# One 2 MB transfer for an expert's gate and up weights in place of two of 1 MB

## The chip, the cores and the metric

The kernel runs on one core of one Trainium2 chip. The metric is the device time of one execution in microseconds (us). Of the kernel before, three runs were timed: 683.28, 684.06 and 685.25 us, the median is 684.06.

## What is computed

One step of a decoder layer over 544 tokens (512 of a prompt, 32 new ones) of width 1024: first a mixer (a spatial gating branch and a recurrent branch, merged by sigmoids and projected), then a mixture of experts, then a norm. The change touches the experts alone. Each of the 32 experts has a gate and an up matrix of 1024 x 256 and a down matrix of 256 x 1024 in float32, and each token goes to two of them:

```python
pg_top, g_idx = lax.top_k(pg, 1)
pe_top, e_idx = lax.top_k(pe, TOP_K_INNER)          # 2 of the 8 experts of the group
h = jax.nn.silu(jnp.einsum('td,edf->tef', xf, w_gate)) * jnp.einsum('td,edf->tef', xf, w_up)
h = h * gates.astype(h.dtype)[..., None]
y = jnp.einsum('tef,efd->td', h, w_down)
```

## The kernel before

The mixer takes the first 375 us or so. Its projection weights come in transfers of 512 KB over the queue of SyncE (SP).

Then routing builds a table of token numbers, and the experts are worked off in pairs. A pair G is two experts with up to 64 tokens each, which lie in the two halves of the 128 partitions. 16 pairs cover the 32 experts; an expert with over 64 tokens gets an extra pair with one half only. The inputs give one such extra, so there are 17 pairs, G = 0 to 16, and the extra one is G = 15.

For a pair, GpSimd gathers 128 token rows of 4 KB from DRAM into `xg` (`gather`, L538). TensorE transposes them (`transposes`, L1434), multiplies by gate and up (L1445: eight steps `c` of the inner dimension for two halves are 16 calls, which the trace shows as 32 matmuls), ScalarE and VectorE make `hm`, TensorE transposes that (L1456) and multiplies by down (L1466), ScalarE evicts to `yo` (L753), and GpSimd scatters the rows of `yo` to DRAM (`scatter`, L548). TensorE's order is written out: gate and up of G, transposes of G+1, down of G, gate and up of G+1, and so on. GpSimd's order is: wait for the transposes of G+1, gather G+2, wait for `yo` of G, scatter G, wait until that has landed, next G. The buffers `xg` and `yo` exist once.

The weights lie in `wslot[q][s]`: q = 0 to 2 are three slots for pairs, s is the half. An expert's 24 KB per partition are contiguous in DRAM: 16 KB of gate and up, interleaved by inner step `c`, and 8 KB of down. They come over SP's queue in the three parts of `PARTS`, each 1 MB in 128 rows of 8 KB: `c` 0 to 3, `c` 4 to 7, down. Six experts are loaded ahead (`expert`, L398): two near 115 us, one near 323 us, one near 367 us, one at 376 us, the last at 403.5 us. Afterwards `refill` (L440) refills the slot of each finished pair, part by part: it waits for `gu_half` (TensorE is past `c` = 3), loads part 0 of both experts, waits for `gu_mm` (past `c` = 7), loads part 1 of both, waits for `pair_mm` (past down), loads both down parts. `further` (L456) does the same for the one expert of the extra pair. Each part has its semaphore, and TensorE waits for part 0 ahead of `c` = 0, for part 1 ahead of `c` = 4 and for the down part ahead of L1466.

SP issues in program order, and the rows of one queue are worked off in order by the 16 DMA engines. The gathers and scatters have a queue of their own, which GpSimd fills, on the same 16 engines.

Behind the last pair, SP loads all of `ytok` back (`gy`), and VectorE, ScalarE and the stores make the output.

Of the kernel before, what the change touches and what calls it, by code (L numbers as in the profile page):

```python
# [97 lines left out]
def build(nc, x, wmix, wgate, chan, wst, bs, rows, wr, br, wmoe, y, vp, vs, st):  # L98
# [9 lines left out]
    GU = KT * 512  # L108
    EW = GU + 2 * D
# [124 lines left out]
    with ExitStack() as ctx:  # L234
        ps = ctx.enter_context(nc.psum_tensor("ps", [P, 8, 512], F32))

        def sem(name):
            return ctx.enter_context(nc.semaphore(name))
# [3 lines left out]
        const_in = sem("const_in")  # L242
        raw_in = [sem(f"raw_in{s}") for s in range(RAW)]

        part_in = [[[sem(f"part{n}_in{q}{s}") for s in range(2)] for q in range(3)] for n in range(3)]
        gw_in = sem("gw_in")
        xres_in = sem("xres_in")
        bd_in = sem("bd_in")
# [73 lines left out]
        coly_copied = sem("coly_copied")  # L322
        xgT_mm = sem("xgT_mm")
        xgT_sb = sem("xgT_sb")
        gu_half = sem("gu_half")
        gu_mm = sem("gu_mm")
        silu_done = sem("silu_done")
        hm_ready = sem("hm_ready")
# [2 lines left out]
        pair_mm = sem("pair_mm")  # L331
# [22 lines left out]
            return ([0, 1, 2, 5], 6, 4) if half == 0 else ([7, 3, 0, 1], 2, 2)  # L354

        TB = (5, 7, 4, 6, 5, 7, 4, 6)
        PARTS = ((0, GU // 2), (GU // 2, GU), (GU, EW))
        ZB = (4, 5, 2, 3)
        XB = (4, 6, 4, 6, 4, 6, 7, 3)

# [2 lines left out]
        def _(sp_):  # L363
# [31 lines left out]
            def expert(q, s, n):  # L395

                for part, (lo, hi) in enumerate(PARTS):
                    e.dma_start(wslot[q][s][:, lo:hi], wmoe[n][:, lo:hi]).then_inc(part_in[part][q][s], 16)  # L398
# [33 lines left out]

            def refill(q, count, number):

                for part, used in enumerate((gu_half, gu_mm, pair_mm)):
                    lo, hi = PARTS[part]
                    e.wait_ge(used, count)
                    e.sem_inc(held, 1)
                    for s in range(2):
                        e.dma_start(wslot[q][s][:, lo:hi], wmoe[bass.ds(number + s, 1), :, lo:hi].rearrange(  # L440
                            "a p c -> (a p) c")).then_inc(part_in[part][q][s], 16)

            with e.Fori(0, 4) as i:
                for q in range(3):
                    refill(q, i * 3 + (q + 1), i * 6 + (6 + 2 * q))
# [3 lines left out]

            def further(count, m):  # L450
                ex = e.value_load(nxi[0:1, bass.ds(m + 1, 1)], min_val=0, max_val=NE - 1)
                for part, used in enumerate((gu_half, gu_mm, pair_mm)):
                    lo, hi = PARTS[part]
                    e.wait_ge(used, count)
                    e.sem_inc(held, 1)
                    e.dma_start(wslot[0][0][:, lo:hi], wmoe[bass.ds(ex, 1), :, lo:hi].rearrange(  # L456
                        "a p c -> (a p) c")).then_inc(part_in[part][0][0], 16)

            with e.If(nx > 0):
                further(PAIRS - 3, 0)  # L460
            refill(1, PAIRS - 2, NE - 2)
            with e.If(nx > 1):
                with e.Fori(1, nx) as m:
                    further(m + (PAIRS - 1), m)
# [722 lines left out]
        def _(pe):  # L1187
# [241 lines left out]
            def transposes(G):  # L1429

                pe.wait_ge(xg_in, G * 16 + 16)
                pe.wait_ge(xgT_sb, FIRST + G)
                for c in range(KT):
                    l = pe.transpose(ps[:, c // 4, (c % 4) * P:(c % 4 + 1) * P], xg[:, c * P:(c + 1) * P], ident[:])  # L1434
                l.then_inc(xgT_mm, 1)

            def pair(G, q, halves, weights_in, next_rows):
                pe.wait_ge(xgT_sb, FIRST + G + 1)
                pe.wait_ge(hm_ready, FIRST + G)
                for c in range(KT):  # L1440
                    if c % 4 == 0:
                        for s in halves:
                            pe.wait_ge(part_in[c // 4][q][s], weights_in)
                    for s in halves:
                        l = pe.matmul(ps[CAP * s:CAP * s + CAP, 2, :], xgT[:, c, CAP * s:CAP * s + CAP],  # L1445
                                      wslot[q][s][:, c * 512:(c + 1) * 512], start=c == 0, stop=c == KT - 1,
                                      tile_position=(0, CAP * s), skip_group_check=True)
                    if c == 3:
                        l.then_inc(gu_half, 1)
                l.then_inc(gu_mm, 1)  # L1450
                if next_rows:
                    transposes(G + 1)
                pe.wait_ge(hm_ready, FIRST + G + 1)
                pe.wait_ge(hT_sb, FIRST + G)
                for f in range(2):
                    l = pe.transpose(ps[:, 3, f * P:(f + 1) * P], hm[:, f * P:(f + 1) * P], ident[:])  # L1456
                l.then_inc(hT_mm, 1)
                pe.wait_ge(hT_sb, FIRST + G + 1)
                for s in halves:
                    pe.wait_ge(part_in[2][q][s], weights_in)  # L1460
                pe.wait_ge(yo_sb, FIRST + G)
                for f in range(2):
                    for h in range(2):
                        for s in halves:
                            o = GU + f * D + h * 512
                            l = pe.matmul(ps[CAP * s:CAP * s + CAP, 6 + h, :], hT[:, f, CAP * s:CAP * s + CAP],  # L1466
                                          wslot[q][s][:, o:o + 512], start=f == 0, stop=f == 1,
                                          tile_position=(0, CAP * s), skip_group_check=True)
                l.then_inc(pair_mm, 1)

            transposes(0)
            with pe.Fori(0, PAIRS // 3) as i:
                for q in range(3):
                    pair(i * 3 + q, q, (0, 1), i * 16 + 16, True)
            pe.wait_ge(extra_ready, 1)
            nx = pe.value_load(nxi[0:1, 0:1], min_val=0, max_val=EXTRA)
            with pe.If(nx > 0):
                with pe.Fori(0, nx) as m:
                    pair(m + (PAIRS - 1), 0, (0,), m * 16 + 16 * (PAIRS // 3 + 1), True)
            pair(nx + (PAIRS - 1), 1, (0, 1), 16 * (PAIRS // 3 + 1), False)  # L1480


# [55 lines left out]
```

## Time and profile before

| | us |
|---|---|
| median of three runs | 684.06 |
| the profiled execution | 682.99 |
| its span | 681.0 |
| around the span | 1.99 |
| TensorE matmul busy | 572.9 |
| VectorE, ScalarE, GpSimd busy | 295.5, 242.6, 64.0 |
| share of 16 DMA engines used by SP's queue | 53.5% |
| mean granted TensorE clock, share of full | 0.941 |

The table is of one execution, taken by the hardware profiler. A line of the page's second part has 40 digits, one for each fortieth of the span (17.0 us); a digit is the busy share in tenths. A matmul counts as busy from its start to a modelled end, so that a busy TensorE is not one at its peak. A wait is put down to what released it last. In rows such as `407.06 8.58 PE L1445` the numbers are the start in us from the span's start and the length in us; in brackets stands how long the engine had been idle before and what ended that. "MATMUL x32" is a run of 32 merged instructions.

### The profile page before, as it was taken

How to read it: one execution, taken by the hardware profiler on the slowest of the kernel's cores; microseconds unless marked ns; L12 is line 12 of the kernel's file. 1: busy time of each engine (PE TensorE's matmuls, PEld its weight loads, DVE VectorE, ACT ScalarE, POOL GpSimd, SP SyncE). 2: the span in 40 equal slices, each digit the busy share in tenths (PEclk: the TensorE clock that was granted, in tenths of full speed). 3: DMA queues.
4: the chain of work that ended last, by engine and by line, in shares of the span. 5: the costliest groups of instructions: out<-in, count | busy, mean ns of one | idle time of the engine just before them, and what ended most of it. 6: DMA issues, size and time to landing. Idle time of an engine off the chain costs nothing.

```text
span 681.0 us, 8485 instructions
## 1 busy us (share of the span) xinstructions
PE 572.9 (84%) x2668; PEld 342.4 (50%) x2668; DVE 295.5 (43%) x583; ACT 242.6 (36%) x386; POOL 64.0 (9%) x137
## 2 busy tenths in 40 slices
PE   3899899999999999999998129898888988889800
PEld 3666497777778777777665113333333323223300
DVE  4824667767767667676323740110011000001138
ACT  5323324464573754654133401222222221112222
POOL 1100070000000000000000011112211221111000
PEclk9899999999999999999999659989999998889965
DMA  9322233921223222311903929999999999999464
GB/s 310 120 66 89 66 115 133 391 101 62 72 69 98 92 69 92 100 62 54 385 1 142 359 103 395 418 422 420 420 420 422 420 420 422 421 420 417 174 247 173
DMA packets 32001, 156.31 MB, mean 230 GB/s; under 512 B 6160, under 2 KB 6544, under 8 KB 19312
## 3 DMA queue, kind: packets, MB, share of 16 engines
q1 hardware_dynamic: 25744, 143.10, 53.5%
q0 software_dynamic: 5472, 10.63, 4.3%
q10 hardware_dynamic: 768, 2.38, 0.9%
q8 instruction: 9, 0.15, 0.1%
q14 instruction: 8, 0.07, 0.0%
HBM read 150.82 MB, written 14.17 MB: 242 GB/s over the span
## 4 chain that ended last, share of the span: by engine, by line
PE 55%; DMA 15%; SPq 15%; DVE 8%; issue 3%; ACT 3%; POOLq 0%; POOL 0%; DVEq 0%; ACTq 0%
PE ps L1192 13%; SPq L440 13%; PE ps L1194 12%; PE ps L1193 12%; DMA wslot<-in_wmoe 4%; DMA ytok<-yo,coly 4%; DMA xg<-xnd,colg 4%; PE ps L1466 3%; PE ps L1219 2%; PE ps L1308 2%; PE ps L1340 2%; DVE x L1173 2%; PE ps L1445 2%; SPq L456 1%; PE ps L1292 1%
## 5 line engine op out<-in xcount | busy, mean ns | idle before, releaser
L1445 PE MATMUL ps<-wslot,xgT 128*64 128x512 f32 x528 | 128.3, 621 | 11.4 <-DMA wslot<-in_wmoe 9.8
L589 ACT ACTIVATE wh<-raw 128x1024 fp32r<-128x1024 f32 x48 | 50.8, 1059 | 171.5 <-PE ps L1194 100.0
L1192 PE MATMUL ps<-xh,wh 128*128 128x512 f32 x256 | 102.5, 401 | 0.0
L1194 PE MATMUL ps<-xl,wh 128*128 128x512 f32 x256 | 100.0, 391 | 0.0
L1193 PE MATMUL ps<-xh,wl 128*128 128x512 f32 x256 | 99.9, 390 | 0.0
L1148 DVE TENSOR_TENSOR hm<-hs,ps 128x256 f32<-128x256 f32 x17 | 7.2, 421 | 197.0 <-ACT hs L748 197.0
L1445 PEld LDWEIGHTS ps<-wslot,xgT 128*64 128x64 f32 x528 | 42.2, 143 | 93.9 <-issue 93.9
L774 DVE TENSOR_TENSOR wl<-raw,wh 128x1024 fp32r<-128x1024 f32 x48 | 59.4, 1238 | 62.4 <-ACT wh L589 61.5
L1466 PE MATMUL ps<-wslot,hT 128*64 128x512 f32 x264 | 65.5, 627 | 8.3 <-ACT hT L750 8.3
L1192 PEld LDWEIGHTS ps<-xh,wh 128*128 128x128 f32 x256 | 48.1, 188 | 16.1 <-issue 6.7
L1194 PEld LDWEIGHTS ps<-xl,wh 128*128 128x128 f32 x256 | 48.1, 188 | 10.5
L1193 PEld LDWEIGHTS ps<-xh,wl 128*128 128x128 f32 x256 | 48.2, 188 | 9.4
L748 ACT ACTIVATE hs<-ps 128x256 f32<-128x256 f32 x17 | 6.5, 383 | 105.8 <-PE ps L1445 105.8
L753 ACT ACTIVATE yo<-ps 128x1024 f32<-128x1024 f32 x17 | 17.4, 1024 | 67.4 <-PE ps L1466 67.4
L1466 PEld LDWEIGHTS ps<-wslot,hT 128*64 128x64 f32 x264 | 19.2, 142 | 43.7 <-issue 31.4
L1434 PE MATMUL ps<-ident,xg 128*128 128x128 f32 x136 | 19.5, 288 | 16.9 <-DMA xg<-xnd,colg 16.9
L1434 PEld LDWEIGHTS ps<-ident,xg 128*128 128x128 f32 x136 | 15.3, 145 | 30.5 <-DMA xg<-xnd,colg 25.6
L1192 PE MATMUL ps<-wh,xh 128*128 128x512 f32 x64 | 27.3, 427 | 2.8 <-DVE xs L800 2.1
L1143 DVE TENSOR_TENSOR xgT<-ps,ch 128x1024 f32<-128x1024 f32 x17 | 20.8, 1225 | 19.5 <-PE ps L1434 19.5
L1192 PE MATMUL ps<-wh,mh 128*128 128x512 f32 x64 | 25.9, 405 | 0.2 <-DVE x L964 0.2
L1193 PE MATMUL ps<-wh,xl 128*128 128x512 f32 x64 | 26.0, 406 | 0.0
L1194 PE MATMUL ps<-wl,xh 128*128 128x512 f32 x64 | 25.9, 405 | 0.0
(290 smaller groups left out, 746.7 us busy)
## 6 DMA issues: line engine op xcount, KB each, us to landing
wslot<-in_wmoe SPq DMA_DIRECT2D x99, 1024.0 KB, 23.9
raw<-in_wmix SPq DMA_DIRECT2D x48, 512.0 KB, 3.6
gy<-ytok SPq DMA_DIRECT2D x8, 512.0 KB, 6.4
xt<-in_x SPq DMA_DIRECT2D x4, 512.0 KB, 7.1
x<-in_x SPq DMA_DIRECT2D x4, 512.0 KB, 4.8
xnd<-xn ACTq DMA_DIRECT2D x4, 512.0 KB, 9.1
out_y<-xn SPq DMA_DIRECT2D x4, 512.0 KB, 2.6
gw<-in_wgate POOLq DMA_DIRECT2D x8, 128.0 KB, 2.4
```

The lines of the kernel that those rows point to most:

```text
L440: e.dma_start(wslot[q][s][:, lo:hi], wmoe[bass.ds(number + s, 1), :, lo:hi].rearrange("a p c -> (a p) c")).then_inc(part_in[part][q][s], 16)
L589: a.activation(wh[:, hslot, :], raw[:, slot, :, :].rearrange("p k c -> p (k c)"), ACT.Copy).then_inc(hi_ready, 1)
L753: a.activation(yo[:], ps[:, 6:8, :].rearrange("p b c -> p (b c)"), ACT.Copy).then_inc(yo_sb, 1)
L774: d.tensor_tensor(wl[:, hslot, :], raw[:, slot, :, :].rearrange("p k c -> p (k c)"), wh[:, hslot, :].bitcast(F32), ALU.subtract).then_inc( ...
L1143: d.tensor_tensor(xgT[:], ps[:, 0:2, :].rearrange("p b (k c) -> p (b k) c", c=P), ch[:, :, C_G2:C_G2 + 1].broadcast_to([P, KT, P]), ALU.mu ...
L1173: d.scalar_tensor_tensor(out=x1[0:r, t, :], in0=gy[0:r, s, t, :], scalar=gate[0:r, s, t:t + 1], in1=x1[0:r, t, :], op0=ALU.mult, op1=ALU.a ...
L1192: pe.matmul(out, sh, mh_, start=start, stop=False)
L1193: pe.matmul(out, sl, mh_, start=False, stop=False)
L1194: return pe.matmul(out, sh, ml_, start=False, stop=stop)
L1434: l = pe.transpose(ps[:, c // 4, (c % 4) * P:(c % 4 + 1) * P], xg[:, c * P:(c + 1) * P], ident[:])
L1445: l = pe.matmul(ps[CAP * s:CAP * s + CAP, 2, :], xgT[:, c, CAP * s:CAP * s + CAP], wslot[q][s][:, c * 512:(c + 1) * 512], start=c == 0, st ...
L1466: l = pe.matmul(ps[CAP * s:CAP * s + CAP, 6 + h, :], hT[:, f, CAP * s:CAP * s + CAP], wslot[q][s][:, o:o + 512], start=f == 0, stop=f == 1 ...
```

## The change

`PARTS` has two entries in place of three: 16 KB per partition of gate and up, and 8 KB of down. So an expert comes in a transfer of 2 MB with 128 rows of 16 KB and one of 1 MB with 128 rows of 8 KB. The semaphore `gu_half` and its increment go, and both gate and up parts of a slot are reloaded after `gu_mm`. TensorE waits once, ahead of `c` = 0. The bytes, the slots and the order of everything else stay.

```diff
-        part_in = [[[sem(f"part{n}_in{q}{s}") for s in range(2)] for q in range(3)] for n in range(3)]
+        part_in = [[[sem(f"part{n}_in{q}{s}") for s in range(2)] for q in range(3)] for n in range(2)]
-        gu_half = sem("gu_half")
-        PARTS = ((0, GU // 2), (GU // 2, GU), (GU, EW))
+        PARTS = ((0, GU), (GU, EW))
             def refill(q, count, number):
-                for part, used in enumerate((gu_half, gu_mm, pair_mm)):
+                for part, used in enumerate((gu_mm, pair_mm)):
             def further(count, m):
-                for part, used in enumerate((gu_half, gu_mm, pair_mm)):
+                for part, used in enumerate((gu_mm, pair_mm)):
             def pair(G, q, halves, weights_in, next_rows):
                 for c in range(KT):
-                    if c % 4 == 0:
+                    if c == 0:
                         for s in halves:
-                            pe.wait_ge(part_in[c // 4][q][s], weights_in)
+                            pe.wait_ge(part_in[0][q][s], weights_in)
...
-                    if c == 3:
-                        l.then_inc(gu_half, 1)
                 l.then_inc(gu_mm, 1)
...
-                    pe.wait_ge(part_in[2][q][s], weights_in)
+                    pe.wait_ge(part_in[1][q][s], weights_in)
```

## Rows read from the trace of the kernel before

**Rows 1.** The page: TensorE and DMA busy tenths, GB/s, in 40 slices

```profile
PE   3899899999999999999998129898888988889800
...
DMA  9322233921223222311903929999999999999464
GB/s 310 120 66 89 66 115 133 391 101 62 72 69 98 92 69 92 100 62 54 385 1 142 359 103 395 418 422 420 420 420 422 420 420 422 421 420 417 174 247 173
```

**Rows 2.** Waits from 400 us on: engine, line, released by; total us, times, longest

```profile
POOL colg L540 <- DMA ytok<-yo,coly: 93.6, 11, 9.2
...
PE ps L1434 <- DMA xg<-xnd,colg: 16.9, 8, 7.7
...
PE ps L1445 <- DMA wslot<-in_wmoe: 9.8, 7, 2.5
```

**Rows 3.** TensorE's timeline: transposes L1434 of G = 1, 2, 11 and gate/up L1445

```profile
407.06 8.58 PE L1445 MATMUL ps<-wslot,xgT 128*64 128x512 f32 x32 [1.60 <-DVE xgT L1143]
415.57 1.09 PE L1434 MATMUL ps<-ident,xg 128*128 128x128 f32 x8
...
427.94 1.09 PE L1434 MATMUL ps<-ident,xg 128*128 128x128 f32 x8
...
551.52 1.09 PE L1434 MATMUL ps<-ident,xg 128*128 128x128 f32 x8 [1.05 <-DMA xg<-xnd,colg]
```

**Rows 4.** TensorE's timeline later: L1434 of G = 13, 14, 16, and waits of L1445

```profile
585.54 1.10 PE L1434 MATMUL ps<-ident,xg 128*128 128x128 f32 x8
...
597.04 5.35 PE L1445 MATMUL ps<-wslot,xgT 128*64 128x512 f32 x16 [2.50 <-DMA wslot<-in_wmoe]
602.32 1.09 PE L1434 MATMUL ps<-ident,xg 128*128 128x128 f32 x8
...
629.29 1.09 PE L1434 MATMUL ps<-ident,xg 128*128 128x128 f32 x8
...
638.53 3.65 PE L1445 MATMUL ps<-wslot,xgT 128*64 128x512 f32 x16 [0.25 <-DMA wslot<-in_wmoe]
```

**Rows 5.** Chain of work, 455 to 500 us: start, length, what

```profile
470.04 1.09 PE ps L1434 x8
...
471.83 3.68 PE ps L1466 x16
475.53 1.03 ACT yo L753
...
477.86 9.23 DMA ytok<-yo,coly
...
488.76 8.27 DMA xg<-xnd,colg
...
497.07 1.09 PE ps L1434 x8
```

**Rows 6.** The gather issued at 399.4 us: from issue to landing

```profile
DMA to landing us min/median/max: 4.0/4.0/4.0
```

**Rows 7.** The gather issued at 475.2 us, and all 17 gathers: from issue to landing

```profile
L543 POOL DMA_INDIRECT xg<-xnd,colg x1: 1037/1037/1037, 475.2 to 475.2; - x1
...
DMA to landing us min/median/max: 8.8/8.8/8.8
...
DMA to landing us min/median/max: 4.0/8.3/8.8
```

**Rows 8.** Transfers of gw (128 rows of 1 KB) issued at 115.0 and 142.0 us

```profile
DMA to landing us min/median/max: 6.4/6.4/6.4
...
DMA to landing us min/median/max: 2.3/2.3/2.3
```

**Rows 9.** Stretches: us; busy of PE, PEld, DVE, ACT, POOL; clock, DMA share, GB/s

```profile
408.00:410.00 2.00, 2.00 (x8) 0.73 (x6) 0.00 (x0) 0.00 (x0) 0.00 (x0) 0.50 1.01 426
412.00:414.00 2.00, 2.00 (x12) 0.77 (x10) 0.00 (x0) 0.00 (x0) 0.00 (x0) 1.00 0.88 271
...
480.00:500.00 20.00, 16.64 (x86) 6.56 (x84) 3.29 (x4) 3.84 (x6) 2.40 (x4) 1.00 1.02 421
```

**Rows 10.** SP's timeline, 402 to 413 us: the last preload and the first refill

```profile
403.51 1.28 SPq L398 DMA_DIRECT2D wslot<-in_wmoe  x3
412.47 0.34 SPq L440 DMA_DIRECT2D wslot<-in_wmoe  x1
```

**Rows 11.** Refills issued from 500 to 590 us: SP's time for one, issue to landing

```profile
L440 SPq DMA_DIRECT2D wslot<-in_wmoe x32: 332/2265/6664, 502.8 to 588.0; - x32
...
DMA to landing us min/median/max: 28.2/30.6/34.5
```

## The prediction

> **What bounds the kernel now.** I read the slices first [rows 1]: the change acts from 400 us on, where DMA stands at 9 and moves 417 to 422 GB/s through twelve slices. TensorE is also at 9 there, so the two have to be told apart, and the waits do that [rows 2]: matmuls waited for weights 7 times, 9.8 us in all, the transposes for gathered rows in 8 waits (7.7 us of them the very first), and GpSimd spent 93.6 us waiting for its own scatters. Then I read TensorE's timeline. From G = 1 (415.57) to G = 11 (551.52) the ten pairs take 13.6 us each and no gate/up waits for weights; the pair ends on the transposes, which wait for the gather [rows 3]. TensorE alone could do a pair in 12.4 us (G = 1 to G = 2, without a wait). Later pairs wait for weights ahead of `c` = 4 and take 16.8 us (585.54 to 602.32), until the last load lands and the last half of gate/up starts at 638.53 after a wait of 0.25 us only [rows 4].
>
> So there are two limits: a loop of gather and scatter, 13.6 us a pair, while the preloaded slots last, and the DMA stream after that. A pair's weights are 6 transfers of 1.05 MB, 14.9 us at 421 GB/s [rows 9]; gather and scatter are 1.05 MB more if every row counts, 2.5 us. That brackets the 16.8. SP is far ahead: refills issued from 502 us on land 28 to 34 us later, and SP itself is held up to 6.7 us in issuing one [rows 11].
>
> **The gather and scatter loop.** The rows of one turn are: a gather issued at 475.22 lands 8.8 us later, at 484.0 [rows 7]; the scatter issued at 477.86 lands at 487.1, thus 3.1 us behind the gather, since both use one queue [rows 5]; 1.7 us later, at 488.76, GpSimd issues the next gather. 8.8 + 3.1 + 1.7 = 13.6. TensorE's part (transposes, down, `yo`) runs beside the gather. The loop is therefore paced by how long 4 KB rows need on engines that are full of weight rows. The gather that met an idle DMA took 4.0 us, the median one 8.3 us [rows 6, 7]: 4.3 us more. The small load `gw` shows the same, 2.3 us alone and 6.4 us beside 8 KB weight rows, 4.1 us more [rows 8]. Both have 8 rows per DMA engine. At 421 GB/s over 16 engines a row of 8 KB lasts 0.311 us, so 8 small rows that each let one weight row pass lose 2.5 us; the other 1.8 us passes ahead of the first small row. This is the reading on which the forecast rests: the queues take turns row by row. (The Trainium skill, DMA: Bandwidth & Descriptors, section Queues, rings and completion order, has each DMA engine go round the queues it has work for and switch only between packets. If its packet of 9 to 17 descriptors were the unit, a change of row size would cost as much again ahead of the first row; no row here tells the two apart.)
>
> **The change, part by part.**
>
> 1. Rows of 16 KB pass in the small rows' gaps, 0.62 us each in place of 0.31. A gather that meets only such rows is longer by 8 x 0.31 = 2.5 us at least, and by the full 4.3 us if the part ahead of the first row grows too. The scatter's landing behind the gather grows by 2.5 us. So the loop would be 13.6 + 5.0 = 18.6 us (up to 20.4). Two thirds of the weight bytes come in such rows: 13.6 + 2/3 x 5.0 = 16.9 us, and 18.1 us with the upper price. No row shows 16 KB rows; the lower bound is no growth at all (13.6, a rival below). This is above the mean engine's work, 14.9 + half of 2.5 = 16.1 us, so backlog no longer builds up, the stream runs dry for a part of each period, and small rows then wait for nothing. With a loop of 6.6 us on an idle DMA (4.0 + 0.9 + 1.7; the 0.9 is an estimate, the slowest engine's eight rows at half weight and some landing), 7.0 us more when 8 KB rows are always there and 12.0 to 13.8 us more when 16 KB rows are, a period p with 5.4 us of the one and 10.7 us of the other solves p = 6.6 + (7.0 x 5.4 + 12.0 x 10.7) / p, 16.6 us, and 17.3 us with the upper price. Should gathers fall mostly beside down weights, p comes to about 15. I take 16.5.
>
> 2. The transposes of G = 1 stand at 415.57, just behind gate/up of G = 0. Their gather runs beside the last preloaded expert, now in 16 KB rows: up to 2.5 us later, I take 2.0, thus 417.6.
>
> 3. From G = 1 to G = 14, 13 periods of 16.5 = 214.5 us, to 632.1. The last refill is issued as gate/up and down of G = 13 end, so the gather of G = 15 still meets it (15 us), that of G = 16 hardly (12.4 us, TensorE's own). The transposes of G = 16 start at 659.5, where they started at 629.29: 30.2 us later. Weights are there by then, which saves the 0.25 us. Behind it nothing changes.
>
> 4. Both gate and up parts are refilled after `gu_mm` in place of `gu_half`. The first refill was issued at 412.47, halfway through gate/up that ends at 415.64 [rows 3, 10]: 3.2 us later now, at a place where the DMA had already a gap (0.88 busy at 412 to 414) [rows 9]. In the stream's limit it costs 3.2 us; under the longer loop it is hidden, as there is 16.1 us of work for 16.5. What is queued behind this wait on SP is the down refill, which waits for a later event anyway.
>
> 5. TensorE waits ahead of `c` = 0 for all 16 KB. For the last pair, whose second part landed last, that puts the first 16 matmuls, 3.5 us (half of 7.0), behind the landing. Again a cost of the stream's limit alone; in the forecast the landing is early.
>
> 6. 33 transfers and as many SP issues fewer. SP waits anyway, so nothing. One end price per row saved is bounded by the best stretch, 426 against 421 GB/s [rows 9]: 1.2% of the 226 us from 412 to 638, 2.7 us, hidden by the loop; at least zero.
>
> 7. The mixer: loads ahead of 400 us carry the same bytes with slack of many us behind them. Nothing.
>
> 8. With 4 us of idle time a pair TensorE may start some transposes and downs at the lower clock, as the gate/up of 5.35 us in place of 3.6 did behind a wait of 2.5 us [rows 4]. About 2 us a pair, beside the gather: nothing, unless the loop is shorter than I think.
>
> Sum: 681.0 + 30.2 - 0.25 = 710.9 us of span, 712.9 with the 1.99 around it. The median of the runs lies 1.07 above the profiled 682.99, so 714 us. Ends: with 17.3, a start at 418.1 and 15.5 and 12.8 for the last two pairs the transposes of G = 16 are at 671.3, 42 us late: 726; some clock loss on top, 730. With 15 they are at 640.0, the stream's limit and TensorE's end nearly meet, and 695 results.
>
> **The rivals.**
>
> - Rows of 16 KB don't hinder small rows more than 8 KB ones (the hardware cuts them, or takes turns in finer steps). Then the loop stays and the stream's limit decides: + 3.2 (point 4) + 3.5 (point 5) - 0 to 2.7 (point 6), that is 688 to 691. It speaks for this that no row here is over 8 KB; against it, that the 4 KB rows do wait for whole 8 KB rows.
> - Faster: the larger transfer pays by its rate, and both late starts are hidden by SP's backlog of 30 us. By 426 GB/s it is 2.7 us: 681.4. The first refill has no backlog ahead of it, however, and the last landing has nothing behind it. It decides once the stream gains more than 6.7 us, 3%. (The Trainium skill, DMA: Bandwidth & Descriptors, section Anatomy of one DMA, fits 2.0 us per transfer plus its bytes at 436 GB/s; 27 transfers fewer in this stretch would be 54 us less, 630 us, as an estimate. The trace speaks against it: back to back, a transfer of 1 MB takes 2.5 us in all at 421 GB/s, where the fit has 4.4.)
> - No difference: gain and late starts cancel within 2 us.
>
> **How the numbers follow.** The forecast, a loop of 15.8 to 17.5 us, 705 to 730 us: 0.47. The same mechanism weaker, 691 to 705: 0.14. The stream's limit alone, 686.2 to 691: 0.22. No difference: 0.07. Faster: 0.08. Over 730: 0.02. A measurement can tell 0.3%, 2 us, from no change. Slower is thus 0.85, same 0.07, faster 0.08. The range from 686 to 730 leaves out 0.17.
>
> **What the profile after would show.** Right: the transposes of neighbouring G stand 16 to 17 us apart from G = 1 on, each after a wait of some 4 us for the gather; gathers beside weights take 11 to 13 us (median 8.3 now); no matmul waits for weights; SP is held less in issuing and waits at `gu_mm`; DMA falls under 9 in slices behind 410 us. Wrong: gathers at 8 to 9 us, a period of 13.6 with SP's backlog as before, and the gate/up of the last pair starting once, at about 638 to 642 us, after a wait for weights. The forecast fails altogether if 16 KB rows are cut into smaller ones.

## The result, and the profile after

The changed kernel takes 705.57 us (median of four runs, 702.31 to 709.18) beside 684.65 for the kernel before on the same chip: a ratio of 1.031, 95% interval 1.028 to 1.035, so 21 us slower. The forecast was 714. The profiled execution took 705.42, its span is 703.7, 22.7 us over the 681.0 of before. One run of experiment 1 and one of the kernel before beside it (731.36 and 722.16 us, at a granted clock of 0.82) are slow ones and are left out of what is said below.

The waits from 400 us on, as in [rows 2]:

```profile
POOL colg L539 <- DMA ytok<-yo,coly: 147.9, 14, 12.7
...
PE ps L1433 <- DMA xg<-xnd,colg: 45.2, 15, 7.9
```

TensorE's waits for weights (9.8 us in seven) have gone altogether. In their place the transposes wait for the gather of nearly every pair, 45.2 us in place of 16.9, and GpSimd waits 147.9 us for its scatters, where it was 93.6. The timeline has the starts of L1433 (L1434 of before) for G = 1, 2, 10, 14, 15 and 16 and the last gate/up, as in [rows 3, 4]:

```profile
416.30 1.09 PE L1433 MATMUL ps<-ident,xg 128*128 128x128 f32 x8
...
429.61 1.09 PE L1433 MATMUL ps<-ident,xg 128*128 128x128 f32 x8 [0.88 <-DMA xg<-xnd,colg]
...
560.58 1.59 PE L1433 MATMUL ps<-ident,xg 128*128 128x128 f32 x8 [3.43 <-DMA xg<-xnd,colg]
...
626.25 1.09 PE L1433 MATMUL ps<-ident,xg 128*128 128x128 f32 x8 [1.59 <-DMA xg<-xnd,colg]
...
639.30 1.09 PE L1433 MATMUL ps<-ident,xg 128*128 128x128 f32 x8 [0.75 <-DMA xg<-xnd,colg]
...
651.53 1.09 PE L1433 MATMUL ps<-ident,xg 128*128 128x128 f32 x8
...
656.55 7.40 PE L1444 MATMUL ps<-wslot,xgT 128*64 128x512 f32 x31
```

The pairs stand 16.15 us apart from G = 1 to G = 14 (209.95 / 13). The first of these 13 distances is 13.3 us and the last 15.35; the eleven between them are 16.5 us on average. The transposes of G = 16 start at 651.53 in place of 629.29: 22.2 of the 22.7 us are there. The last gate/up runs through without a wait for weights.

The chain of work of 545 to 580 us shows one turn of the loop, as in [rows 5]:

```profile
552.66 12.74 DMA ytok<-yo,coly
...
567.07 10.18 DMA xg<-xnd,colg
...
577.30 1.26 PE ps L1433 x8
```

The gather of the same turn, issued at 549.9 us, and below it all gathers, then the refills issued from 500 to 590 us (SP's time for one, then issue to landing), as in [rows 7, 11]:

```profile
L542 POOL DMA_INDIRECT xg<-xnd,colg x1: 1034/1034/1034, 549.9 to 549.9; - x1
...
DMA to landing us min/median/max: 10.7/10.7/10.7
```

```profile
DMA to landing us min/median/max: 4.2/10.6/12.0
```

```profile
L439 SPq DMA_DIRECT2D wslot<-in_wmoe x22: 185/333/333, 501.9 to 584.9; - x22
...
DMA to landing us min/median/max: 13.2/17.2/23.2
```

The gather of 549.9 lands at 560.6, the scatter at 565.4, 4.8 us later, and GpSimd issues the next gather at 567.07, 1.7 us after that: 10.7 + 4.8 + 1.7 = 17.2 us. It was 8.8 + 3.1 + 1.7. Both are single turns, and the new one is among the longest. GpSimd's timeline gives the mean of many: the changed kernel's gathers of G = 3 and G = 14, and the same of the kernel before for G = 3 and G = 12:

```profile
434.61 1.04 POOL L542 DMA_INDIRECT xg<-xnd,colg  x1 [0.87 <-POOL colg L539]
...
616.26 1.04 POOL L542 DMA_INDIRECT xg<-xnd,colg  x1 [0.86 <-POOL colg L539]
```

```profile
433.81 1.04 POOL L543 DMA_INDIRECT xg<-xnd,colg  x1 [0.87 <-POOL colg L540]
...
556.82 1.03 POOL L543 DMA_INDIRECT xg<-xnd,colg  x1 [0.86 <-POOL colg L540]
```

These are 16.5 us a turn (181.65 / 11) and 13.7 (123.01 / 9). Taking issues and landings of all these turns one by one, a gather lands 10.8 us after its issue (before 8.4), the scatter 4.1 us behind the gather (before 3.6), and GpSimd needs 1.7 us more (before 1.7). So nearly all of the growth, 2.4 of 2.8 us, is in the gather.

SP is no longer held up in issuing (333 ns, before up to 6.7 us), and refills land after 17 us in place of 31: the backlog is about half. It is not gone, as none of these refills lands sooner than 13.2 us after its issue. DMA is full, as the page's slices of 17.6 us show (the row as in [rows 1]); from 422 us on it moves 409 to 426 GB/s for eleven slices, to 616 us. The slice ahead of them stands at 7, as the first refill is issued at 416.6 us and was at 412.5:

```profile
DMA  8221324722222222207309379999999999987064
GB/s 315 102 88 63 113 82 188 306 90 67 89 97 67 89 97 67 89 30 286 140 16 362 123 287 422 426 421 425 422 422 425 425 421 416 409 306 283 2 245 163
```

### The profile page after: what moved, and what is told of

It reads as the page before. It is cut to its first block, busy times and chain, and to the rows that moved or that the text cites. A ratio compares the mean times of both kernels' runs of the same rounds, so it can differ in the third digit from the quotient of the medians.

```text
span 703.7 us, 8372 instructions
## 1 busy us (share of the span) xinstructions
PE 576.4 (82%) x2668; PEld 344.0 (49%) x2668; DVE 295.7 (42%) x583; ACT 242.8 (34%) x386; POOL 64.6 (9%) x137
## 3 DMA queue, kind: packets, MB, share of 16 engines
q1 hardware_dynamic: 20992, 143.10, 51.5%
## 4 chain that ended last, share of the span: by engine, by line
PE 58%; DMA 25%; DVE 7%; issue 4%; ACT 4%; POOL 1%; POOLq 1%; SPq 0%; DVEq 0%; ACTq 0%
PE ps L1191 13%; DMA ytok<-yo,coly 13%; PE ps L1193 12%; PE ps L1192 12%; DMA xg<-xnd,colg 10%; PE ps L1463 6%; PE ps L1444 3%; PE ps L1218 2%; PE ps L1307 2%; PE ps L1339 2%; PE ps L1433 2%; DVE x L1172 1%; ACT yo L752 1%; PE ps L1291 1%; DMA gy<-ytok 1%
## 5 line engine op out<-in xcount | busy, mean ns | idle before, releaser
L1444 PE MATMUL ps<-wslot,xgT 128*64 128x512 f32 x528 | 122.0, 599 | 1.6 <-DVE xgT L1142 1.6
L1444 PEld LDWEIGHTS ps<-wslot,xgT 128*64 128x64 f32 x528 | 39.5, 138 | 80.2 <-issue 80.2
L1463 PE MATMUL ps<-wslot,hT 128*64 128x512 f32 x264 | 71.4, 675 | 8.0 <-ACT hT L749 8.0
L1433 PE MATMUL ps<-ident,xg 128*128 128x128 f32 x136 | 22.2, 315 | 45.2 <-DMA xg<-xnd,colg 45.2
L1193 PEld LDWEIGHTS ps<-xl,wh 128*128 128x128 f32 x256 | 48.1, 188 | 10.6
L1433 PEld LDWEIGHTS ps<-ident,xg 128*128 128x128 f32 x136 | 17.0, 157 | 59.2 <-DMA xg<-xnd,colg 58.4
L749 ACT ACTIVATE hT<-ps 128x256 f32<-128x256 f32 x17 | 6.5, 383 | 57.1 <-PE ps L1453 57.1
```

The source lines that it names most:

```text
L1193: return pe.matmul(out, sh, ml_, start=False, stop=stop)
```

## The experiments

**1. The waits of the changed kernel with rows of 8 KB.** Two transfers of 1 MB, both issued after `gu_mm`, both awaited ahead of `c` = 0:

```diff
-                for part, used in enumerate((gu_half, gu_mm, pair_mm)):
+                for part, used in enumerate((gu_mm, gu_mm, pair_mm)):
...
-                    if c % 4 == 0:
+                    if c == 0:
                         for s in halves:
-                            pe.wait_ge(part_in[c // 4][q][s], weights_in)
+                            pe.wait_ge(part_in[0][q][s], weights_in)
+                            pe.wait_ge(part_in[1][q][s], weights_in)
```

> Gate and up of an expert come as two transfers of 1 MB with rows of 8 KB, as in the kernel before, but both are issued after gu_mm, and TensorE waits for both ahead of c = 0: the waits are those of the changed kernel, the rows those of the kernel before. Theory (rows of 16 KB hold up the small rows): gathers land in 8.3 us again, the pairs stand 13.6 us apart until the weight stream binds, and the time is that of the stream's limit with the two late starts of 3.2 and 3.5 us, 688 to 692 us. Rival (the late refill and the single wait make the loss, the gathers are only a sign of it): about 705 us, as the changed kernel.

Measured: 692.32 us (median of three runs), ratio to the kernel before 1.011 (1.007 to 1.016). Its gathers:

```profile
DMA to landing us min/median/max: 3.8/8.3/8.7
```

The theory holds, with a time 0.3 us above its range: gathers land as before, and the pairs stand 13.4 us apart from G = 1 to G = 8 (93.6 / 7). About a third of the loss, 7.7 us by the ratio, is in the two waits, the rest is in what differs between this kernel and the changed one: the form of the transfer.

**2. One transfer of 2 MB, in rows of 8 KB.** The weights lie in DRAM with a gap of 256 B after each 8 KB, so that the rows of a transfer can't be joined. This parts the length of a row from the size of a transfer:

```diff
+        CUT, PAD = 2, 64
+        RUN = GU // CUT
...
+            return e_[0].dma_start(slot[:, 0:GU].rearrange("p (a c) -> p a c", a=CUT),
+                                   row[:, 0:CUT * (RUN + PAD)].rearrange("p (a c) -> p a c", a=CUT)[:, :, 0:RUN])
...
-                    e.dma_start(wslot[q][s][:, lo:hi], wmoe[n][:, lo:hi]).then_inc(part_in[part][q][s], 16)
+                    load(wslot[q][s], wmoe[n], part).then_inc(part_in[part][q][s], 16)
```

> One transfer of 2 MB as in the changed kernel, same waits, but the weights lie in DRAM with a gap of 256 B after 8 KB, so that the transfer consists of 256 rows of 8 KB. Theory (the length of a row counts, not the size of a transfer): gathers of 8.3 us, 688 to 692 us, the same as with two transfers of 8 KB rows. Rival (queues take turns by whole transfers or by a fixed number of rows, so that a transfer of 2 MB holds up a gather whatever its rows): gathers of 10 to 11 us and about 705 us. If neighbouring rows were joined again, the trace would show it in the count of packets.

Measured: 692.02 us, 1.012 (1.009 to 1.015). The packets of SP's queue are 20992 in the changed kernel and here, by the list of queues,

```profile
q1 hardware_dynamic: 25216, 143.10, 52.7%
```

which is 4224 more, one for each of the 33 x 128 rows that were cut in two. The gathers' median is 8.4 us (10.6 in the changed kernel). So a transfer of 2 MB does no harm as such; its rows of 16 KB do.

This alone rules out turns of whole transfers, and not turns of a fixed number of rows, which the expectation names together with them. The trace's records of single rows tell these apart. They don't name the DMA engine. Which row follows which is therefore an estimate: ends and starts within about 10 ns of each other are counted, less those that fall together by chance. Of the 1103 rows of 4 KB on GpSimd's queue from 440 to 560 us of the kernel before, 86% are followed at once by a weight row and 1% by another row of their own; in the changed kernel it is 90% and none. In the kernel before, 90% of the weight rows that stand behind a row of GpSimd's queue are followed by one of that queue again. So the two queues take turns row by row here.

**3. The same with rows of 4 KB** (CUT = 4).

> As the kernel with one transfer of 2 MB in rows of 8 KB, but with rows of 4 KB for gate and up (down stays at 8 KB). Theory: a gather beside rows of 4 KB loses half as much as beside 8 KB, by 2/3 of the weights: 8.3 - 2/3 x 2.1 = 6.9 us; the pairs come down to TensorE's own 12.4 us as long as preloaded slots last. The end is set by the stream's limit, which pays for the shorter rows: 688 to 700 us, and no gain from the faster gathers. Rival (the gathers' latency does not depend on row length): 8.3 us.

Measured: 696.69 us, 1.019 (1.016 to 1.022). All gathers, and the stretch of 560 to 600 us:

```profile
DMA to landing us min/median/max: 4.3/8.0/8.6
```

```profile
560.00:600.00 40.00, 31.70 (x148) 12.01 (x146) 4.94 (x6) 6.92 (x10) 6.07 (x10) 0.91 1.02 413
```

The time is in the range, but the step downward is not what was expected: 8.0 us and not 6.9. A small row does not simply lose the time of one row of the other queue at every length. From 8 to 4 KB the gather gains 0.3 us where 1.4 was due; from 8 to 16 KB it grew by 2.3, where the same two thirds of 2.5 make 1.7. The records of single rows show in which part of a gather this lies: its first row starts 1.8 us after the issue on an idle DMA, and at the median 4.1 to 4.2 us after it beside weight rows of 4, 8 and 16 KB alike. The length of the other queue's rows acts behind that: from the first row to the landing it is 2.2 us alone and 3.8, 4.1 and 6.5 us beside rows of 4, 8 and 16 KB. Why 4 KB gives no more was not found. The stream itself moves 413 GB/s where rows of 8 KB give 421, 2% of some 226 us, 4.4 us, and this is about what lies between the 692.0 and the 696.7.

**4. The changed kernel with the loop cut.** Rows of 16 KB stay; GpSimd issues gather G+3 ahead of its wait for scatter G (the core of the edit; the first turn stands ahead of the loop):

```diff
+            def landed(total):
                 g.wait_ge(y_out, total)
                 g.sem_inc(yo_free, 1)
...
                 gather(bass.ds(G + 2, 1), G + 3)
+                landed(G * 16)
                 g.wait_ge(yo_sb, FIRST + G + 1)
...
-                scatter(bass.ds(G, 1), G + 1, G * 16 + 16)
+                scatter(bass.ds(G, 1), G + 1)
```

> The changed kernel with GpSimd's order altered alone: the wait for scatter G to land stands behind the issue of gather G+3 instead of ahead of it. Rows of 16 KB stay. Theory (a serial loop of gather, scatter and gather sets the pace of the changed kernel): the loop is cut, a gather is issued 2.4 us after the transposes that free its buffer and lands 10 to 12 us later, the pairs stand 13 to 14.5 us apart until the stream binds, and the time falls to the stream's limit, 686 to 692 us. Rival (the DMA engines lose throughput to 16 KB rows, or TensorE's lower clock makes the loss): it stays at 700 to 706 us.

Measured: 691.45 us, 1.010 (1.007 to 1.013), 14 us less than the changed kernel. Gathers still take 10.4 us at the median. TensorE's timeline (L1442 is L1433 there; G = 1, 8 and 12) and the weights' rate:

```profile
416.72 1.09 PE L1442 MATMUL ps<-ident,xg 128*128 128x128 f32 x8
...
507.51 1.09 PE L1442 MATMUL ps<-ident,xg 128*128 128x128 f32 x8 [0.49 <-DMA xg<-xnd,colg]
...
574.43 1.09 PE L1442 MATMUL ps<-ident,xg 128*128 128x128 f32 x8
```

```profile
500.00:560.00 60.00, 48.68 (x211) 18.33 (x208) 4.94 (x6) 11.79 (x15) 8.47 (x14) 0.91 1.01 425
```

13.0 us a pair (90.8 / 7) up to G = 8, then 16.7 (66.9 / 4) with waits for weights. So it was the serial loop, not the rows' rate, nor TensorE's clock (0.91 granted from 500 to 560 us, and 0.94 in the changed kernel): a gather as slow as in the changed kernel does no harm once it is issued early. What is left over the kernel before, 6.6 us by the ratio, is near the 7.7 of the two waits, which this kernel has too.

**5. The late refill alone**: the kernel before with the first of the two edits of experiment 1.

> The kernel before with one edit: both gate and up parts are reloaded after gu_mm. Rows of 8 KB, two transfers, and TensorE still waits for the second part ahead of c = 4 only. Theory: the weight stream starts 3.2 us later with nothing queued ahead of it, and binds afterwards, so 3 to 4 us more than before (1.005). Rival (SP's backlog hides it): no difference.

Measured: 687.35 us beside 683.81, 1.0048 (1.003 to 1.0067): 3.3 us by the ratio, as expected.

**6. The single wait alone**: the kernel before with the second edit of experiment 1.

> The kernel before with one edit: TensorE waits for both gate and up parts ahead of c = 0. The refills stay as early as before, rows of 8 KB. Theory: behind the last landing stand 32 matmuls in place of 16, so 3 to 4 us more than before (1.005); pairs 11 to 14, which wait for weights too, lose nothing that adds up, since the stream sets their distance. Together with the late refill it makes the 7 to 8 us of the kernel with both. Rival: it costs at each of the five pairs that wait, or holds back the refills, over 6 us.

Measured: 688.15 us beside 683.81, 1.0059 (1.0039 to 1.0078): 4.0 us. 3.3 + 4.0 are 7.3 of the 7.7 us of experiment 1. But the place was not the one forecast. The wait that counts is that of G = 14, here and in the kernel with both edits (L1446 is L1445 in both):

```profile
614.31 8.78 PE L1446 MATMUL ps<-wslot,xgT 128*64 128x512 f32 x32 [4.22 <-DMA wslot<-in_wmoe]
```

```profile
616.94 9.51 PE L1446 MATMUL ps<-wslot,xgT 128*64 128x512 f32 x32 [4.85 <-DMA wslot<-in_wmoe]
...
643.76 7.40 PE L1446 MATMUL ps<-wslot,xgT 128*64 128x512 f32 x31
```

The last pair has its weights in time. At G = 14, two pairs before the last, TensorE waits 4.22 and 4.85 us, has all 32 matmuls behind the landing in place of 16, and its clock has fallen meanwhile (8.78 and 9.51 us for what takes 7.0; 0.79 granted from 616 to 630 us of the second kernel); from there to the end it waits for no weights.

**7. The kernel before with GpSimd's new order.**

> The kernel before with GpSimd's order altered alone (gather G+3 is issued ahead of the wait for scatter G). Theory: the loop of 13.6 us a pair falls to TensorE's 12.4 to 13 us, so pairs use up the preloaded slots sooner and meet the stream's limit sooner; the end is set by the stream, no difference within 0.3%. Rival (the loop costs time in the kernel before too): 3 us or more faster.

Measured: 683.71 us beside 683.81, 0.999 (0.997 to 1.001). The starts of the transposes (L1443 is L1434 there) for G = 1, 8, 9, 16:

```profile
415.59 1.09 PE L1443 MATMUL ps<-ident,xg 128*128 128x128 f32 x8
...
502.18 1.09 PE L1443 MATMUL ps<-ident,xg 128*128 128x128 f32 x8
516.01 1.09 PE L1443 MATMUL ps<-ident,xg 128*128 128x128 f32 x8
...
629.40 1.09 PE L1443 MATMUL ps<-ident,xg 128*128 128x128 f32 x8
```

12.37 us a pair for seven pairs (86.59 / 7), TensorE's own pace, 8 us ahead of the kernel before at G = 8, and none of it is left at G = 16 (629.40 against 629.29). In the kernel before, the loop costs nothing; the stream decides.

**8. 16 KB rows with both late starts undone.** Experiment 4, with the first refill and that of the last pair in halves of 8 KB rows.

> The changed kernel with GpSimd's new order, and with the two late starts undone where they cost: the first refill and that of the last pair come in halves (8 KB rows, one issued after gu_half and one after gu_mm; the last pair waits for its second half ahead of c = 4). All other transfers are of 2 MB with 16 KB rows. Theory: 3.2 and 3.5 us come back of the 691.5 us that the kernel with the new order took, so 684 to 686 us, level with the kernel before; if the 16 KB rows' higher rate (425 against 421 GB/s) reaches the end, up to 2 us less, 682 to 684.

Measured: 685.89 us beside 683.81, 1.0024 (1.0005 to 1.004). By the ratios (1.0097 and 1.0024) 5.0 of the 6.6 us come back. The rate of 424 to 425 GB/s gives no lead: G = 14 still waits for its 16 KB at once, and its 32 matmuls take 8.78 us:

```profile
611.71 8.78 PE L1471 MATMUL ps<-wslot,xgT 128*64 128x512 f32 x32 [2.08 <-DMA wslot<-in_wmoe]
```

**9. What the stream's limit consists of.** The stream ends raggedly in the kernel before; from 630 us on the mean share of the 16 DMA engines that is in use (the last number but one) falls step by step:

```profile
630.00:634.00 4.00, 3.53 (x14) 1.40 (x14) 1.46 (x2) 0.38 (x1) 0.00 (x0) 1.00 0.84 350
634.00:636.00 2.00, 2.00 (x11) 0.71 (x10) 0.00 (x0) 1.10 (x2) 0.00 (x0) 1.00 0.68 285
636.00:638.00 2.00, 2.00 (x10) 0.58 (x6) 0.00 (x0) 1.21 (x1) 0.97 (x2) 1.00 0.42 176
```

Each of the 544 tokens goes to two experts, so that on average 64 of the 128 places of a pair are taken. The tokens fill a half from its first partition on, so that, on the reading to be tested, some engines carry most of the gathered rows and come last with every weight transfer. The trace's semaphore events fit this: the 16 parts of each of the last weight transfers (one for each DMA engine), which land at 633.5 to 643.8 us, are 17 us apart. The edit (the table of positions is written with ranks dealt out over the slots):

```diff
-            d.tensor_tensor(posh[:, 0:TILES, :], row(iota[:], TILES), bc(posv[:, 0:TILES], P), ALU.is_equal).then_inc(pos_ready, 1)
+            for h in range(2):
+                i = d.tensor_tensor(
+                    posh[:, 0:TILES, CAP * h:CAP * h + CAP].rearrange("p t (c x) -> p t x c", x=4),
+                    iota[:, CAP * h:CAP * h + CAP].rearrange("p (t x c) -> p t x c", t=1, x=4).broadcast_to([P, TILES, 4, 16]),
+                    posv[:, 0:TILES].rearrange("p (t x c) -> p t x c", x=1, c=1).broadcast_to([P, TILES, 4, 16]), ALU.is_equal)
+            i.then_inc(pos_ready, 1)
```

> The kernel before; only the partition a token's row takes within its half is altered. Ranks are dealt out, rank r going to slot 4 * (r mod 16) + r div 16, where they filled the half from its first partition on. So the valid rows of a gather or scatter fall evenly on the 16 DMA engines. Theory (the stream's limit is that of the DMA engine with most gathered rows; in the kernel before the 16 parts of the last weight transfers land up to 17 us apart, and the last of them sets the end): the last landing comes some 7 us sooner, 676 to 680 us. Rival (the spread of landings has another cause): no difference.

Measured: 678.21 us beside 683.51, 0.993 (0.991 to 0.996). The same stretches as above:

```profile
630.00:634.00 4.00, 4.00 (x19) 1.46 (x17) 0.00 (x0) 2.31 (x2) 0.74 (x2) 1.00 1.01 421
634.00:636.00 2.00, 1.95 (x10) 0.71 (x10) 0.00 (x0) 0.00 (x0) 0.44 (x1) 1.00 0.96 401
636.00:638.00 2.00, 2.00 (x12) 0.56 (x8) 0.00 (x0) 0.00 (x0) 0.00 (x0) 1.00 0.87 354
```

The engines stay busy nearly to the end, and this is the fastest kernel of the study, 5 us under the kernel before. The 16 parts of the last weight transfers are now 5 to 6 us apart, and the last one lands at 639.7 us, 4.1 us sooner, where some 7 were expected.

**10. The changed kernel with tokens dealt out.**

> The changed kernel with tokens dealt out over the DMA engines in the same way. Theory (the loop of gather and scatter sets its pace): a gather has 8 rows on each engine before and after, with a place beyond the tokens costing only its turn, so the loop gets shorter only by the 4 KB rows that the fullest engine no longer has, some 0.5 us a gather and as much a scatter: 10 to 15 us less, 690 to 697 us. Rival (the stream sets its pace): down by 7 us as the kernel before, 698 us.

Measured: 700.6 us beside 683.51, 1.026 (1.023 to 1.028). By the ratios (1.031 and 1.026) 4 us less than the changed kernel, fewer than either theory had. The gathers' median is 10.5 us (10.6): what a gather loses lies in the turns, and not in its own rows on the fullest engine. The 4 us are in the loop all the same, and more in the scatters. These are the eleven scatters from 437 us on, in the changed kernel and here:

```profile
L552 POOL DMA_INDIRECT ytok<-yo,coly x11: 1009/1013/1025, 437.4 to 603.7; - x11
...
DMA to landing us min/median/max: 8.9/12.1/13.1
```

```profile
L552 POOL DMA_INDIRECT ytok<-yo,coly x11: 1012/1017/1029, 439.4 to 599.1; - x11
...
DMA to landing us min/median/max: 9.5/11.1/12.5
```

A turn, from one gather's issue to the next, takes 16.04 us over the same eleven turns (436.44 to 612.93), where it was 16.51: the gather is 0.2 us shorter and the scatter's landing behind it 0.3. Eleven times that is 5 us.

**11. The kernel before with both, new order and tokens dealt out.**

> The kernel before (8 KB rows, three parts) with GpSimd's new order and the tokens dealt out. Theory: the new order alone changed nothing since the stream bound; with the stream 7 us shorter it is still the stream that binds, so 676 to 680 us, at most 1 us below the kernel with the tokens dealt out alone.

Measured: 678.83 us beside 683.51, 0.994 (0.992 to 0.996), level with dealing out alone. The stream still decides.

**12. 16 KB rows with everything**: experiment 8 and tokens dealt out.

> 16 KB rows in all but the first and the last refill, GpSimd's new order, tokens dealt out. Theory: if the 16 KB rows' rate (425 against 421 GB/s) counts at the end once the engines are level, 2 us below the same kernel with 8 KB rows, 674 to 678 us; the single wait ahead of c = 0 at the pairs 13 to 15 that wait for weights speaks against it. Rival: level with it or up to 2 us above, as the kernel with split ends was against the kernel before.

Measured: 682.32 us beside 683.51, 0.998 (0.997 to 1.000), 3.5 us above the same with 8 KB rows (2.9 by the ratios), more than even the rival allowed. Two pairs near the end, G = 13 and G = 14, wait for all of gate and up at once, and gate/up takes 8.5 and 8.8 us behind the wait in place of 7.0, at a lower clock:

```profile
590.63 8.47 PE L1481 MATMUL ps<-wslot,xgT 128*64 128x512 f32 x32 [3.50 <-DMA wslot<-in_wmoe]
...
606.78 8.78 PE L1481 MATMUL ps<-wslot,xgT 128*64 128x512 f32 x32 [2.19 <-DMA wslot<-in_wmoe]
```

So with the loop cut, both ends in halves and the tokens dealt out, transfers of 2 MB are no gain here. The single wait at the pairs between stays in this kernel, as one transfer has one landing; whether it makes all of the 3 us was not tested.

## Why the prediction was right, and where it was off

The mechanism was the forecast one. Rows of 16 KB lengthen the gathers, the loop of gather and scatter takes over from the weight stream as the limit, and no wait for weights is left. Experiments 1 and 2 show that it is the rows, experiment 4 that it is the loop. The size was 30 us where it is 21. The middle of the forecast comes from the right loop by a working in which two parts are off and partly cancel, as the points below show.

- Point 1, the gather: 10.6 us at the median; the prediction's signs said 11 to 13. Growth is 2.3 us (2.4 over the turns of the loop). Weighted by two thirds, the prediction's prices were 1.7 and 2.9. The part ahead of the first small row did not grow with the row (4.1 to 4.2 us beside 8 and 16 KB), so that part of the upper price is out; behind it a gather lost nearly the full 2.5.
- Point 1, the scatter: its landing behind the gather was to grow by 2.5 us beside 16 KB rows, 1.7 weighted. It grew by 0.4 on average over the loop's turns (3.6 to 4.1). This is the part of the turn that was sized wrongly.
- Point 1, the dry stream: a turn above the mean engine's work was to leave the stream dry for a part of each period, which took the 16.9 to 18.1 us of the plain sum down to 16.6 to 17.3. In stretches of 4 us from 420 to 612 us the DMA share is never under 0.97, and no refill issued from 500 to 590 us lands sooner than 13.2 us after its issue. Only from the gather of 549.9 on do first rows come 2.4 to 3.6 us after the issue in place of 4.2, which fits a few engines that have run out of weight rows. So the turn of 16.5 us was met with too large a scatter and a dryness that was not there to that extent: the 16.5 itself is in part luck.
- Points 1 and 3, the period: 13 times 16.5 us was taken, the result is 16.15 on average. The loop ran at 16.5, but it does not set the first distance, G = 1 to G = 2 (13.3 us, the gather of G = 2 waits for no scatter), and the last is 15.35. The average is 4.6 us of the miss, the largest term, and these two distances make 4.4 of it: the number of turns was off, not their length.
- Point 2: the transposes of G = 1 were to come 2.0 us later by a longer gather. They started at 416.30, 0.73 us later, and so did those of G = 0 (0.74): nothing came from the gather. 1.3 us of the miss.
- Point 3, the last two pairs: 15 and 12.4 us were taken, 13.05 and 12.23 came. 2.1 us of the miss. The three terms together are 8.0 us: 659.5 was forecast for the transposes of G = 16, 651.53 measured. The tail behind them is 0.7 us longer than forecast, and the 3.1 us that the forecast adds to the span (1.99 around it, 1.07 from the profiled execution to the median) are 1.9 in the changed kernel: 8.0 - 0.7 + 1.2 is the whole miss of 8.4 us, to rounding.
- Point 4, the late refill: priced at 3.2 us for the stream's limit and hidden under the longer loop. Alone, in the kernel before, it costs 3.3 us. That it is hidden in the changed kernel was not tested by itself.
- Point 5, the single wait: priced at 3.5 us, it costs 4.0, but at G = 14 and through the clock too, not behind the last landing.
- Point 6: the gain by rate was bounded by 2.7 us. Rates are 425 for 16 KB rows, 421 for 8 KB; no kernel of the study turned that into time.
- Point 8, the clock: transposes of 1.5 to 1.6 us in place of 1.1 at G = 8 to 10, beside the gather, as forecast.
- A sign was wrong: between 422 and 616 us, where the loop is the limit, DMA did not fall under 9 tenths. It stands lower only in the slice of the first refill (7) and behind 616 us (8 and 7, then the stream's end), where the last refills wait for their pairs. What did shrink is the backlog.
- A reading of [rows 1] was off: TensorE stands at 8 in nine of the twelve slices, and not at 9. The waits, by which the prediction parted the two limits, are read rightly.

The rival on the stream's limit (688 to 691 us) came out as the time of the kernels with the loop unharmed, 692.3, 692.0 and 691.5 us: its sum of 6.7 us was about one short. The faster rival had no share: neither transfer size nor fewer issues gave anything. (The Trainium skill, DMA: Bandwidth & Descriptors, section Rules for kernel authors, asks for 1 MiB or more per DMA for full bandwidth. The trace agrees with 1 MB as enough: 421 GB/s both with 1 MB transfers and, in experiment 2, with 2 MB ones of the same rows.)

What stays open: why rows of 4 KB beside a gather save it so little, what holds up the first row of a gather by some 2.4 us (4.2 in place of 1.8) beside weight rows of any of the three lengths, and why the scatter's landing behind the gather grew so much less than the gather.

## What to carry to other kernels

When a transfer is merged, look at the length of its rows and at who else uses the DMA engines: small gathers on another queue pay for the longer rows, and a serial chain of them can become the limit while the large stream looks as healthy as ever. A merged transfer also merges two waits: the buffer is refilled later and its consumer starts later, each for half a step. And the stream's end was set here by its fullest DMA engines: the share in use fell off slowly (0.84, 0.68, 0.42), and levelling the load was worth 5 us, more than any change of transfer size.

## What the runs showed of the hardware

A gather of 128 places of 4 KB, 64 of them taken on average, took 4.0 us alone, 8.3 us beside rows of 8 KB, 10.6 beside rows of 16 KB, 8.0 beside rows of 4 KB (in the last two a third of the weight bytes came in rows of 8 KB); the size of the other transfer, 1 or 2 MB, made no difference (8.3 and 8.4). Its first row started 1.8 us after the issue alone and 4.1 to 4.2 us beside weight rows of each of the three lengths, and the two queues took turns row by row. DMA as a whole moved 413, 421 and 425 GB/s with weight rows of 4, 8 and 16 KB. The places of the tokens among a gather's rows, with the same bytes in all, moved the end of the whole kernel by 5 us.
